# A streaming encoder layer: the first mLSTM head, table loads, split forget sums and the order of a few TensorE pieces

## The reference

```
h = rmsnorm(x);  z = h @ w_in          # q, k, v, gates of three branches
mLSTM:    4 heads of 128, causal conv + SiLU on q/k, exponential input gate,
          sigmoid forget gate with running maximum:
          w[t,s] = exp(cum[t] - cum[s] + ig[s] - m[t]);  sw = (q.k) * w
          num = sw @ v + w_state * (q @ c);  den = sum(sw) + w_state * (q @ n)
          h_m = rmsnorm(num / max(|den|, exp(-m))) * sigmoid(mo);  new c, n, m
forgetting attention: 8 heads of 64, logits += sum of log forget values, causal
memory attention:     4 heads of 128 over 256 memory tokens
x += (sum over branches of sigmoid(gate_b) * (branch_b @ w_up_b)) @ w_out
x += PEER(rmsnorm(x))                  # 16384 one-neuron experts, product keys
y = rmsnorm(x)
```

## Time and profile before

| | |
|---|---|
| median of 3 runs | 1977.38 us (1972.48 to 1977.8) |
| the profiled execution | 1974.42 us, its span 1972.7 us |
| busy share PE, DVE, ACT, POOL | 98%, 74%, 44%, 45% |
| mean granted TensorE clock | 0.993 |
| PE busy, 0 to 40 us | 31.34 us |
| PE busy, 163 to 206 us (first head) | 38.03 of 43 us |
| PE busy, 206 to 240 us (second head) | 31.49 of 34 us |
| PE busy, 330 to 531 us (attention) | 198.92 of 201 us |

### The profile page before, as it was taken

The page is one execution under the profiler, slowest core; times in us unless marked ns, Lnnn a source line. Parts: engine busy times, 40 slices in busy tenths (PEclk is TensorE's granted clock), DMA queues, the critical chain, the costliest instruction groups (busy, mean ns, idle before and its releaser), DMA issues.

```text
span 1972.7 us, 34503 instructions
## 1 busy us (share of the span) xinstructions
PE 1925.8 (98%) x12602; PEld 1213.0 (61%) x12602; DVE 1464.0 (74%) x2955; ACT 864.6 (44%) x1309; POOL 885.2 (45%) x558
## 2 busy tenths in 40 slices
PE   8999999999999999999989999999999999999997
PEld 6646767777777787555555666655555555555554
DVE  7974656464255577988499899963699988899885
ACT  6443446565443343333445666653333333333331
POOL 2732212222233363676767776776344522345320
PEclk9999999999999999999999999999999999999998
DMA  5622113222452222667879999998999998999971
GB/s 199 217 99 89 54 43 113 95 84 85 143 174 95 97 76 90 214 230 261 289 284 348 365 365 373 364 306 300 351 399 403 394 362 329 343 386 392 382 276 49
DMA packets 160906, 469.33 MB, mean 238 GB/s; under 512 B 17353, under 2 KB 59345, under 8 KB 160281
## 3 DMA queue, kind: packets, MB, share of 16 engines
q1 hardware_dynamic: 81680, 240.98, 34.3%
q0 software_dynamic: 41728, 151.03, 20.7%
q10 hardware_dynamic: 37384, 75.84, 10.5%
HBM read 402.98 MB, written 64.80 MB: 237 GB/s over the span
## 4 chain that ended last, share of the span: by engine, by line
PE 91%; issue 2%; POOL 2%; DVE 2%; ACT 2%; DMA 1%; ACTq 0%; DVEq 0%; POOLq 0%; SPq 0%
PE ps L1836 38%; PE ps L2276 28%; PE ps L1946 11%; PE ps L1852 3%; POOL w_lo L584 2%; PE ps L2098 2%; PE ps L2222 1%; PE ps L2223 1%; PE ps L2295 1%; PE ps L2078 1%; PE ps L2156 1%; PE ps L2064 1%; ACT w_hi L694 0%; PE ps L2012 0%; PE ps L2054 0%
## 5 line engine op out<-in xcount | busy, mean ns | idle before, releaser
L584 POOL TENSOR_TENSOR w_lo<-raw,w_hi 128x1024 bf16<-128x1024 f32 x229 | 507.0, 2217 | 675.6 <-ACT w_hi L694 652.6
L694 ACT ACTIVATE w_hi<-raw 128x1024 bf16<-128x1024 f32 x357 | 374.4, 1051 | 383.0 <-PE ps L2276 192.7
L1836 PE MATMUL ps<-act_hi,w_hi 128*128 128x432 bf16 (+1 forms) x1040 | 357.8, 345 | 0.8 <-DVE proj L1191 0.8
L1836 PE MATMUL ps<-act_hi,w_lo 128*128 128x432 bf16 (+1 forms) x1040 | 357.8, 345 | 0.0
L1836 PE MATMUL ps<-act_lo,w_hi 128*128 128x432 bf16 (+1 forms) x1040 | 357.7, 345 | 0.0
L2276 PE MATMUL ps<-W_hi,w_hi 128*128 128x432 bf16 x992 | 343.3, 346 | 0.8 <-issue 0.8
L2276 PE MATMUL ps<-W_hi,w_lo 128*128 128x432 bf16 x992 | 343.3, 346 | 0.0
L2276 PE MATMUL ps<-W_lo,w_hi 128*128 128x432 bf16 x992 | 343.3, 346 | 0.0
L617 POOL DMA_INDIRECT rows<-in_v_units,rowi x128 | 163.4, 1276 | 317.6 <-DVE accS L1733 297.8
L1626 DVE CUSTOM_DVE_ANT_0 rows<-rows,ps 128x1024 f32<-128x1024 f32 x128 | 153.7, 1215 | 86.4 <-DMA rows<-in_u_rows,rowi 85.8
L1046 ACT ACTIVATE hb<-ps 128x432 f32<-128x432 f32 x128 | 67.9, 530 | 307.3 <-PE ps L1836 305.3
(11 more groups left out here) (447 smaller groups left out, 3366.7 us busy)
## 6 DMA issues: line engine op xcount, KB each, us to landing
raw<-in_u_units SPq DMA_DIRECT2D x128, 512.0 KB, 4.5
raw<-in_v_units SPq DMA_DIRECT2D x128, 512.0 KB, 10.7
raw<-in_units SPq DMA_DIRECT2D x99, 512.0 KB, 3.3
hd<-hb ACTq DMA_DIRECT2D x128, 224.0 KB, 5.4
Hb<-hd SPq DMA_DIRECT2D x32, 896.0 KB, 8.7
gd<-gsb ACTq DMA_DIRECT2D x48, 448.0 KB, 7.4
Gb<-gd SPq DMA_DIRECT2D x32, 672.0 KB, 6.9
gz<-stage ACTq DMA_DIRECT2D x24, 288.0 KB, 2.1
```

What stands on the lines that cost most here:

```text
L584: pool.tensor_tensor(w_lo[:, k % RING, :], raw[:, k % RAW, :], w_hi[:, k % RING, :], ALU.subtract).then_inc(lo_ready, 1)
L694: act.activation(w_hi[:, k % RING, :], raw[:, k % RAW, :], ACT.Copy).then_inc(hi_ready, 1)
L1836: last = pe.matmul(ps[:, bank + half, 0:n], w[:, slot, col:col + P], x(k)[:, half * n:(half + 1) * n], start=(k == 0 and w is w_hi and x i ...
```

## The change

1. Memory values: ScalarE's copy of memv is put ahead of the last of four weight conversions. TensorE's groups of mv and fv take the frames in the order 2, 3, sample, 0, 1.
2. The sigmoid of the output gates moves from ahead of the first head to the place behind its third fill copy; a one-column Exp stands where it was and another behind it.
3. In heads 2 to 4 a one-column Sqrt is put ahead of the second fill copy.
4. `split_cum` is called behind the weighing of tiles 1, 2, 3 of the first head, and no longer behind the argument calls of tiles 3, 4, 5.
5. In heads 2 to 4 the first score product goes ahead of the wait for bank 2 and of the broadcast L1985.
6. `gate_pieces`: the first attention item gets two pieces more, and the others share two less.

```diff
+AHEAD = 2
 def gate_pieces(i):
-    n, first, total = (HF + HC) * NTT, 6 * N_PROJ + LEAD, 6 * N_GATE - LEAD
-    return range(first + total * i // n, first + total * (i + 1) // n)
+    n, first, total = (HF + HC) * NTT, 6 * N_PROJ + LEAD, 6 * N_GATE - LEAD - AHEAD
+    return range(first + (AHEAD if i else 0) + total * i // n, first + AHEAD + total * (i + 1) // n)
...
-            for n in range(U_MEMV, U_MEMV + N_MEMV):
+            for n in range(U_MEMV, U_MEMV + N_MEMV - 1):
                 high_unit(n + RING)
+            act.wait_ge(unit_used, U_MEMV + N_MEMV)
             act.activation(mvN[:, :, :], ps[:, 4:6, :], ACT.Copy).then_inc(nat_evac, 1)
+            high_unit(U_MEMV + N_MEMV - 1 + RING)
...
-            act.wait_ge(fill_evac, 2 * PRE_TILES)
-            act.activation(proj[:, MO:MO + HM, :], proj[:, MO:MO + HM, :], ACT.Sigmoid).then_inc(mo_sig, 1)
+            act.activation(warm[:, 2:3], epsb[:, 0:1], ACT.Exp)
...
                     if j == 2:
+                        if h:
+                            act.activation(warm[:, 3:4], epsb[:, 0:1], ACT.Sqrt)
                         fill_out(x0 + 1)
                         if h:
                             head_roots(h - 1)
                     if j == 4:
                         fill_out(x0 + 2)
+                        if h == 0:
+                            act.wait_ge(fill_evac, 2 * PRE_TILES)
+                            act.activation(proj[:, MO:MO + HM, :], proj[:, MO:MO + HM, :], ACT.Sigmoid).then_inc(mo_sig, 1)
+                            act.activation(warm[:, 2:3], epsb[:, 0:1], ACT.Exp)
...
                     weigh(j)
+                    if h == 0 and j < 3:
+                        split_cum(j)
                     if j + 2 < 5:
                         argument(j + 2)
...
-                    if h == 0 and j >= 2:
-                        split_cum(j - 2)
...
-            frames = [(t * P, P) for t in (2, 3, 0, 1)] + [(TP, TS)]
+            frames = [(2 * P, P), (3 * P, P), (TP, TS), (0, P), (P, P)]
...
-                natural(U_MV, u, act_hi, act_lo, frames, [6, 7, 4, 5, 2], [0, 0, 1, 1, 0])
+                natural(U_MV, u, act_hi, act_lo, frames, [6, 7, 2, 4, 5], [0, 0, 0, 1, 1])
...
-                natural(U_FV, u, act_hi, act_lo, frames, [FV_BANKS[t] for t in (2, 3, 0, 1)] + [3], [0, 0, 4, 5, 0])
+                natural(U_FV, u, act_hi, act_lo, frames, [FV_BANKS[2], FV_BANKS[3], 3, FV_BANKS[0], FV_BANKS[1]], [0, 0, 0, 4, 5])
...
-                if h:
-                    pe.wait_ge(m_dve, N_MD * (h - 1) + 7)
-                pe.matmul(ps[:, 2, :], pick, mn3[0:68, 1, 0:TP], start=True, stop=True).then_inc(m_bn, 1)
...
-                scores(0)
+                if h:
+                    scores(0)
+                    pe.wait_ge(m_dve, N_MD * (h - 1) + 7)
+                pe.matmul(ps[:, 2, :], pick, mn3[0:68, 1, 0:TP], start=True, stop=True).then_inc(m_bn, 1)
+                if h == 0:
+                    scores(0)
                 scores(1)
```

## The result

| | before | changed kernel |
|---|---|---|
| median, 4 runs each on one chip | 1976.64 us (1972.48 to 1977.8) | 1957.64 us (1956.55 to 1961.81) |
| ratio, 95% interval | | 0.9912 [0.9898, 0.9926] |
| the profiled execution, its span | 1974.42, 1972.7 us | 1956.58, 1954.8 us |
| mean granted TensorE clock of it | 0.993 | 0.997 |

Forecast was 1960.5 us, in a range from 1953 to 1970, and faster. Both hold.

A forecast was written before the change was run, and what follows sets the result against it. TensorE was taken to bound the kernel, so its standing still costs one for one. The terms summed to 15.7 us off 1974.42 (1958.7), or 1961.7 from the median; forecast 1960.5 us, range 1953 to 1970.

The forecast's parts named there:

- A: Memory values: the earlier memv copy and new group order remove TensorE's 1.53 us wait; 1.7 us, bounds 0 to 1.7.
- B: Ahead of the first head: with the sigmoid moved away, the first exponential starts earlier; 3.25 us, bounds 0 and 3.5.
- C: First head's value products: without the long wait TensorE's clock stays at 2.4 GHz; 1.7 us, bounds 0 and 3.4.
- D: First head: split forget sums moved behind tiles 1 to 3 remove TensorE waits; 1.6 us, bounds -0.3 and 1.75.
- The sigmoid's new place: Behind the first head's third fill copy: 4.9 us block on ScalarE costs nothing, or 1.5 us without cover.
- E: Heads 2 to 4: sqrt table loaded ahead of the fill copy, roots earlier; three times 1.13, 3.4 us, bounds 0 and 3.4.
- F: Heads 2 to 4: first score product runs inside the 0.84 us wait for the states' bank; 2.5 us, bounds 0 and 2.5.
- rival (2): Heads held by ScalarE and VectorE one step on, E and F (5.9 us) becoming waits elsewhere; 1966.4 us, chance 0.10.
- G: First attention item: two more gate pieces fill its 1.50 us wait; 1.6 us, bounds 0.5 and 1.6.
- (1): First head: first split step slow, 1.9 us more wait at the second tile, clock falls again; 1964 us, chance 0.17.
- (3): Second expert loop's 6.3 us wait for hot_lo grows by what comes in early; 1976 us, chance 0.08.
- (4): Second expert loop becomes bound by its loads, each unit 0.2 us late; 1985 us, chance 0.05.

The follow-up runs named there:

- pool_two: gates_tail with GpSimd's subtraction of units 24 to 79 made in two halves of 512 columns; 1955.6 us, 0.9896 of the kernel before.
- frames_old: Changed kernel with the old order of the frames of mv and fv, the memv copy still moved; 1960.43 us, 0.9908 of the kernel before.
- busy_wait: Kernel before with 25 extra matmuls, results thrown away, in the first head's 3.36 us wait; 1976.71 us, 0.9995 of the kernel before.
- sigmoid_old: Changed kernel with the output gates' sigmoid back ahead of the first head; 1962.31 us, 0.9938 of the kernel before.
- gates_tail: Changed kernel with the first attention item's two early gate pieces taken from the last item alone; 1956.97 us, 0.9897 of the kernel before.
- gates_even: Changed kernel with no extra gate pieces in the first attention item (AHEAD = 0); 1958.56 us, 0.9907 of the kernel before.

## Why the prediction was right

**What bounds the kernel**: right. Every microsecond in which TensorE no longer stood was one off the span, up to the merge at 515.80 (531.70 before), and all of them reached the end. The reading of the waits was wrong in one place. "All but a few tenths of them stand where this change works" leaves out 7.9 us for the first weights, 1.6 at the merge, 1.5 and 0.9 in VectorE's lines of projections, 0.6 for mkT and, in the attention stage itself, 0.48 and 0.62. The last two were worth a term: pool_two takes them away.

**A**: right in size; the frames' order, which I took for a part of it, does nothing (frames_old).

**B and C**: right (3.35 and 1.61). That the slow clock followed from standing still is shown by busy_wait, that the wait was the sigmoid's by sigmoid_old.

**D**: right. The narrowing took 0.52 us, since GpSimd was through at 170.38 (168.25 + 2.13), and the second tile came 0.11 late, where I had 0.15 (my own figures, 2.22 less 2.0, give 0.22).

**The sigmoid's new place**: 0 forecast, 0.25 us measured. The 1.5 us of cover held for the absolute values, but I followed only VectorE from there, not the weight conversion behind them on ScalarE, which GpSimd's subtraction hangs on.

ScalarE's own block came out as 1.28 + 2.12 + 1.28 + 0.20 = 4.9 us. The drain of 1380 ns for each switch, which the Trainium skill gives (ScalarE: Activation LUTs, What ACT_TABLE_LOAD costs), does not show in this trace: the sigmoid starts 1.30 us after its load, and the exponential ahead of the first head 1.40 us after its own.

**E**: right in what was held, 3.07 of 3.4. I added 0.17 us of overlap to each wait of 0.97; between these two shapes of matmul it is 0.05.

**F**: the term "F, scores first" was too large, 1.90 of 2.5. The wait went in full, and the second head has its 0.81. In the third and fourth head TensorE's first value product comes 0.2 us late. VectorE holds it back: it works without a break from the states' copy to the first argument (L1363), and in these two heads the low part of an earlier head's norm (L1328) stands in between, so that the argument starts well behind the broadcast. VectorE at the third head, whose broadcast starts at 228.56 and whose first value product starts at 232.84:

```profile
229.09 0.75 DVE L1328 TENSOR_TENSOR proj_b<-proj,proj_b 128x576 bf16<-128x576 f32 x1
229.76 1.27 DVE L1363 TENSOR_SCALAR wk<-ps,cS 128x512 f32<-128x512 f32 x2
...
232.00 0.69 DVE L1375 SCALAR_TENSOR_TENSOR wk<-ps,wk 128x512 f32<-128x512 f32 x1
```

So "all behind it is 0.83 us earlier" held for TensorE's order but not for VectorE's, a small form of rival (2). That moving L1328 would give the 0.2 us back was not run. What the step missed on the other side is 1.67 us: the third boundary no longer drops to 1.2 GHz. I had this as C's upper bound (3.4), and 0 of 33 against 5 of 9 boundaries says that it belongs to F.

**G**: the term "G, gate pieces" failed: with the early pieces attention is 0.22 us longer, not 1.6 shorter, and that is below its lower bound of 0.5. The wait of 1.50 went as described, and the first item ended 0.29 us later (I had 0.35). "Items that go from three pieces to two lose cover which the two-piece items do without" was the wrong sentence: the two-piece items do without it only as long as VectorE's steps don't start beside a subtraction of GpSimd. gates_tail and pool_two show both parts.

**Sum**: my terms measured 12.9 us, 2.8 under the forecast (G 1.8, F 0.6, E 0.3, the sigmoid 0.25, C 0.1, less 0.3 that A, B and D gave over). This was made up by 3.3 us of clock, 0.9 at the front, 0.4 elsewhere in attention and 0.3 at the hot_lo wait. Of these the 1.67 at 530 us, the 0.87 at the front and the 0.3 are not the change's: at 530 us the clock stays up in 6 of 14 profiles, gates_even among them, and falls in 8, and the front holds nothing of the change (the memory values begin at 78.3 to 79.6 us over all profiles). So the right total is in part luck. TensorE's busy time shows it too: down 5.0 us, where I had 1 to 3. Over all runs the mean granted clock rose from 0.992 (29 runs of before) to 0.996 (4 runs): of the 19 us between the medians some 10 are waits and some 8 the clock. Of the clock's part the change can claim C and the last head's boundary, 3.3 us. gates_even and frames_old, with the same heads, have a mean clock of 0.995 only, and medians of 1958.56 and 1960.43 us.

**Rivals**: (1) fell, narrowing 0.52 us and no wait at the second tile. (2) fell but for F's 0.2 us in two heads. (3) fell: the wait for hot_lo went from 6.3 to 6.0 us, and did not grow by what came in early. (4) fell: no wait for a load in the second expert loop, merge to end 1439.0 us (1441.0 before).

## What to carry to other kernels

Where one engine bounds, its waits add up one for one, and a chain that is started earlier (a table loaded in idle time, a long activation moved out of the path) gives about the wait, as long as no other engine's order holds the next step. Work moved up as cover is taken from somewhere: look at the items it leaves, and at which engine's steps will then start beside which. When the edits are worth 2 us each and runs scatter by 4, size them by the distances between fixed steps of the traces, and keep the granted clock apart from the waits. And undo one edit at a time before crediting it: a stage's gain (0.22 us here) can come from elsewhere while the edit made for it loses.

## What the runs showed of the hardware

**VectorE is held by GpSimd.** From 140 to 520 us of the changed kernel, every VectorE copy, cast, scaling or two-input instruction from SBUF to SBUF, of more than one column, that starts with or within a GpSimd subtraction of 2.13 us lasts until that is over. 0.49 became 2.42 us (item 26, also in gates_tail), 0.52 became 2.39 (narrowing, before), and in item 6 a subtraction of 0.74 us (before) took 2.41. The maximum ended 0.6 us behind the subtraction's end in every head. Not all are held: with an input in PSUM the scaling of the turned keys (L1399) took 0.34 us and the low part of an attention output (L1440) 0.28, inside a subtraction or away from one, and the reciprocal (L1315) 1.94 either way. VectorE, then GpSimd, in the changed kernel:

```profile
318.40 2.41 DVE L1460 TENSOR_TENSOR k_even<-proj,k_even 64x576 bf16<-64x576 f32 x1
```

```profile
318.08 2.13 POOL L585 TENSOR_TENSOR w_lo<-raw,w_hi 128x1024 bf16<-128x1024 f32 x1 [8.28 <-ACT w_hi L695]
```

The Trainium skill (GPSIMD Engine Reference, 1. Specifications) says that GpSimd shares its SBUF interfaces with VectorE, with contention for VectorE instructions that have two SBUF inputs or run in one of its fast modes. The traces agree on those with two SBUF inputs (held) and on those with one in PSUM (not held), and give the price, up to 1.9 us a meeting here. Halving the GpSimd instruction gave 3.1 us in attention (pool_two).

**The clock can fall behind short waits.** At the head boundaries the clock fell in 5 of 9 cases, each time behind a wait of 0.83 or 0.84 us; each fall cost about 1.7 us, twice the wait. The length of the wait alone does not decide: the clock fell neither behind the nine waits of 0.97 us for the roots nor behind the three of 1.50 at the first attention item, and behind the same 1.57 us at the merge it fell in 8 of 14 traces.

**Filling a wait does not pay by itself.** With 25 extra matmuls the slow clock left the first head and came at three other places.
